# State space rounds of a hybrid decoder step: each tile's sums, scans and rotation in one round, outputs one round behind

## What is computed

```python
u = (h @ w_in).reshape(bsz, t, S5_GROUPS, S5_GROUP)
bu_re = jnp.einsum('btgi,gpi->btgp', u, bb_re)
bu_im = jnp.einsum('btgi,gpi->btgp', u, bb_im)
...
_, _, x_re, x_im = lax.associative_scan(combine, (a_re_t, a_im_t, bu_re, bu_im), axis=1)
y = (jnp.einsum('gip,btgp->btgi', c_re, x_re) - jnp.einsum('gip,btgp->btgi', c_im, x_im)
     + d_skip * u).reshape(bsz, t, S5_WIDTH)
za, zg = jnp.split(jax.nn.gelu(y).astype(h.dtype) @ w_glu, 2, axis=-1)
return za * jax.nn.sigmoid(zg), x_re[:, -1], x_im[:, -1]
```

## Time and profile before

| | |
|---|---|
| three runs | 1793.01, 1790.54, 1792.56 us; median 1792.56 |
| the profiled execution | 1795.36 us, its span 1793.6 us |
| mean granted clock of TensorE | 0.957 of full speed |
| busy share of the span | TensorE 94%, VectorE 78%, ScalarE 67%, POOL 8% |
| the rounds | from 500.07 us (first lags) to 600.92 us (first GLU product) |

### The profile page before, as it was taken

The page is one execution under the profiler, slowest core; times in us unless marked ns, Lnnn a source line. Parts: engine busy times, 40 slices in busy tenths (PEclk is TensorE's granted clock), DMA queues, the critical chain, the costliest instruction groups (busy, mean ns, idle before and its releaser), DMA issues.

```text
span 1793.6 us, 27141 instructions
## 1 busy us (share of the span) xinstructions
PE 1693.6 (94%) x9199; PEld 1423.5 (79%) x9199; DVE 1395.1 (78%) x1587; ACT 1201.2 (67%) x1499; POOL 149.5 (8%) x199
## 2 busy tenths in 40 slices
PE   6989899999787898999999999999999999999994
PEld 3867789988666877888888888888888888888884
DVE  2564454583587546999999999999899999999997
ACT  2633355403474546888888888888887888888885
POOL 1042000000066102500000000000000000000001
PEclk8998899999886898999999999999999999999997
DMA  8662655436361559999999999999999999999995
GB/s 342 274 239 88 227 209 188 159 129 252 128 249 48 199 210 380 422 410 372 381 369 404 365 371 400 371 388 372 368 411 367 361 409 364 399 383 359 396 371 200
DMA packets 72869, 553.22 MB, mean 308 GB/s; under 512 B 8256, under 2 KB 8527, under 8 KB 15328
## 3 DMA queue, kind: packets, MB, share of 16 engines
q1 hardware_dynamic: 69186, 538.54, 77.4%
q0 software_dynamic: 3072, 12.54, 1.9%
q10 hardware_dynamic: 542, 1.20, 0.2%
HBM read 530.74 MB, written 21.53 MB: 308 GB/s over the span
## 4 chain that ended last, share of the span: by engine, by line
PE 89%; DVE 4%; ACT 2%; DMA 2%; POOL 1%; issue 1%; ACTq 0%; DVEq 0%; POOLq 0%; SPq 0%
PE bank L1957 86%; PE bank L2431 2%; DMA arena<-in_state_conv_dram 1%; DMA ring<-in_dense_rows_dram 1%; POOL plain_hi L763 0%; DVE sq L1372 0%; PE bank L2410 0%; DVE rstd L1354 0%; DVE sq L1525 0%; DVE w_lo L469 0%; DMA fT<-y_rows,row_i 0%; ACT w_hi L463 0%; ACT hT L1201 0%; DVE sq L1501 0%; ACT arena L1180 0%
## 5 line engine op out<-in xcount | busy, mean ns | idle before, releaser
L1957 PE MATMUL bank<-w_hi,parts 128*128 128x512 f32 x3024 | 897.2, 391 | 1.5 <-DVE parts L1879 1.5
L516 DVE TENSOR_TENSOR w_lo<-ring,w_hi 128x1024 fp32r<-128x1024 f32 x654 | 785.2, 1223 | 57.0 <-ACT w_hi L511 18.7
L511 ACT ACTIVATE w_hi<-ring 128x1024 fp32r<-128x1024 f32 x654 | 690.6, 1061 | 154.4 <-PE bank L1957 154.3
L1957 PEld LDWEIGHTS bank<-w_hi,parts 128*128 128x128 f32 x3024 | 563.0, 188 | 115.9 <-issue 1.7
L1957 PE MATMUL bank<-w_lo,parts 128*128 128x512 f32 x1512 | 548.2, 390 | 0.0
L1957 PE MATMUL bank<-parts,w_hi 128*128 128x264 f32 x1600 | 312.6, 297 | 23.8 <-DVE parts L1361 23.8
L1957 PEld LDWEIGHTS bank<-w_lo,parts 128*128 128x128 f32 x1512 | 283.8, 188 | 60.0
L1957 PEld LDWEIGHTS bank<-parts,w_hi 128*128 128x128 f32 x1600 | 261.5, 199 | 34.8 <-issue 22.6
L1957 PE MATMUL bank<-parts,w_lo 128*128 128x264 f32 x800 | 234.2, 293 | 0.0
L469 DVE TENSOR_TENSOR w_lo<-ring,w_hi 128x2048 fp32r<-128x2048 f32 x50 | 114.6, 2296 | 147.0 <-ACT w_hi L463 146.9
L1957 PEld LDWEIGHTS bank<-parts,w_lo 128*128 128x128 f32 x800 | 158.1, 198 | 0.0
(11 more groups left out here) (415 smaller groups left out, 1247.7 us busy)
## 6 DMA issues: line engine op xcount, KB each, us to landing
ring<-in_expert_rows_dram SPq DMA_DIRECT2D x330, 1024.0 KB, 7.3
ring<-in_dense_rows_dram SPq DMA_DIRECT2D x48, 2048.0 KB, 8.1
hT<-in_expert_rows_dram SPq DMA_DIRECT2D x55, 1024.0 KB, 7.3
ring<-in_dense_rows_dram SPq DMA_DIRECT2D x8, 1408.0 KB, 6.0
x_rows<-arena SPq DMA_DIRECT2D x1, 7168.0 KB, 27.7
y_rows<-arena SPq DMA_DIRECT2D x10, 512.0 KB, 9.3
arena<-x_rows SPq DMA_DIRECT2D x9, 512.0 KB, 10.0
ring<-in_dense_rows_dram SPq DMA_DIRECT2D x2, 1024.0 KB, 4.8
```

Source lines behind the costliest of these rows:

```text
L511: act.activation(hi_slots[u % AHEAD], raw_unit(u), ACT.Copy).then_inc(hi_ready, 1)
L516: dve.tensor_tensor(lo_slots[u % AHEAD], raw_unit(u), hi_slots[u % AHEAD].bitcast(F32), ALU.subtract).then_inc(lo_ready, 1)
L1957: return pe.matmul(out, lhsT, rhs, start=start, stop=stop, skip_group_check=True)
```

## The change

Each tile is now turned back, has its lags masked, is scanned and rotated in the same round, and its outputs follow one round behind the sums: VectorE and POOL have eight rounds, TensorE and ScalarE nine. On TensorE `outputs(k - 1)` stand between the turns and the lag products of tile k + 1. On VectorE `lags(k)` stand between `turn_back(k)` and `scans(k)`. On POOL `pad_c` is one tile ahead, and `rotate_re(k)` closes round k. On ScalarE `copy_lags(k + 1)` goes from the place behind `b_mats(k + 1)` to the place behind `gelu(k - 1)`, ahead of the copy of an ada block. Ada block 20 goes to round 7, and of the copies back to the order of time those of tiles 4 to 6 go ahead of the last gelu on ScalarE, and are a set of their own on VectorE.

```diff
--- before.py
+++ after.py
@@ -777,17 +777,17 @@
                 step(pool.tensor_tensor(wk[:, 1, :, :], turn_sin[:, k, :, :], wk[:, 2, :, :], ALU.mult))
                 pool.tensor_tensor(x, x, wk[:, 1, :, :], ALU.subtract).then_inc(xre_ready, 1)
 
-            for k in range(KT + 1):
-                if k < KT:
-                    wk = work[k % 2]
-                    pool.tensor_tensor(decay[k % 2], bview(cols[:, 3, 4 * k:4 * k + 4], [P, 4, CHUNKS], 2),
-                                       bview(not_first, [P, 4, CHUNKS], 1), ALU.mult)
-                    pool.wait_ge(w_used, k + 1)
-                    pool.tensor_tensor(wk[:, 0, :, :], wk[:, 0, :, :], wk[:, 1, :, :], ALU.add)
-                    pool.tensor_tensor(wk[:, 2, :, :], wk[:, 2, :, :], wk[:, 3, :, :], ALU.subtract).then_inc(w_ready, 1)
-                    pad_c(k)
-                if k:
-                    rotate_re(k - 1)
+            pad_c(0)
+            for k in range(KT):
+                wk = work[k % 2]
+                pool.tensor_tensor(decay[k % 2], bview(cols[:, 3, 4 * k:4 * k + 4], [P, 4, CHUNKS], 2),
+                                   bview(not_first, [P, 4, CHUNKS], 1), ALU.mult)
+                pool.wait_ge(w_used, k + 1)
+                pool.tensor_tensor(wk[:, 0, :, :], wk[:, 0, :, :], wk[:, 1, :, :], ALU.add)
+                pool.tensor_tensor(wk[:, 2, :, :], wk[:, 2, :, :], wk[:, 3, :, :], ALU.subtract).then_inc(w_ready, 1)
+                if k + 1 < KT:
+                    pad_c(k + 1)
+                rotate_re(k)
 
             pool.wait_ge(s5_out, 2)
             for i, (a, b) in enumerate(((s5_re_prompt, s5_re_sample), (s5_im_prompt, s5_im_sample))):
@@ -1168,10 +1168,9 @@
             copy_lags(0)
             act.wait_ge(acc_full, TILES["in1"] + KT)
             pad_b(1)
-            for k in range(KT + 2):
+            for k in range(KT + 1):
                 if k + 1 < KT:
                     b_mats(k + 1)
-                    copy_lags(k + 1)
                 if k + 2 < KT:
                     pad_b(k + 2)
                 if k in (1, 2):
@@ -1186,19 +1185,26 @@
                 if k < KT:
                     sample_states(k)
                     k_mats(k)
+                if k:
+                    last_states(k - 1)
+                if k == KT:
+                    act.wait_ge(y_used, KT - 1)
+                    for r in range(2):
+                        for s_ in range(4):
+                            act.activation(*from_chunks(slice(4, 7), r, s_), ACT.Copy)
+                if k:
+                    gelu(k - 1)
+                if k + 1 < KT:
+                    copy_lags(k + 1)
                 if k < 4:
                     ada(16 + k)
-                if 1 <= k <= KT:
-                    last_states(k - 1)
-                if k >= 2:
-                    gelu(k - 2)
-                if k == KT:
+                if k == KT - 1:
                     ada(20)
                     split_dense_hi(act, 42)
             act.wait_ge(y_used, KT)
             for r in range(2):
                 for s_ in range(4):
-                    act.activation(*from_chunks(slice(4, 8), r, s_), ACT.Copy)
+                    act.activation(*from_chunks(slice(7, 8), r, s_), ACT.Copy)
             act.activation(hT[0:QUAD, :, TP:T], y_one[0:QUAD, :, 0, :], ACT.Copy)
             act.activation(hT[QUAD:2 * QUAD, :, TP:T], y_one[0:QUAD, :, 1, :], ACT.Copy).then_inc(y_moved, 1)
             ada(21)
@@ -1759,15 +1765,11 @@
                 step(dve.tensor_tensor(wk[:, 3, :, :], turn_cos[:, k, :, :], wk[:, 2, :, :], ALU.mult))
                 dve.tensor_tensor(x, x, wk[:, 3, :, :], ALU.add).then_inc(xim_ready, 1)
 
-            lags(0)
-            for k in range(KT + 1):
-                if k < KT:
-                    turn_back(k)
-                if k:
-                    scans(k - 1)
-                    rotate_im(k - 1)
-                if k + 1 < KT:
-                    lags(k + 1)
+            for k in range(KT):
+                turn_back(k)
+                lags(k)
+                scans(k)
+                rotate_im(k)
                 if 1 <= k <= 2:
                     dve.wait_ge(acc_free, TILES["in1"] + KT)
                     rows_placed = place_rows(slice(4, 8), k - 1)
@@ -1775,16 +1777,17 @@
                         rows_placed.then_inc(u_second, 1)
                 if 1 <= k <= 4:
                     mod_rows(15 + k)
-                if k >= KT - 1:
+                if k >= KT - 2:
                     dve.wait_ge(y_used, 4)
-                    for r in (2 * k - 14, 2 * k - 13):
+                    for r in (2 * k - 12, 2 * k - 11):
                         for s_ in range(4):
                             dve.tensor_copy(*from_chunks(slice(0, 4), r, s_))
             split_dense_lo(dve, 42)
-            dve.wait_ge(y_used, KT)
-            for r in range(2, 4):
-                for s_ in range(4):
-                    dve.tensor_copy(*from_chunks(slice(4, 8), r, s_))
+            for seen, ks in ((KT - 1, slice(4, 7)), (KT, slice(7, 8))):
+                dve.wait_ge(y_used, seen)
+                for r in range(2, 4):
+                    for s_ in range(4):
+                        dve.tensor_copy(*from_chunks(ks, r, s_))
             for r in range(2, 4):
                 ins = dve.tensor_copy(hT[QUAD * r:QUAD * r + QUAD, :, TP:T], y_one[0:QUAD, :, r, :])
             ins.then_inc(y_moved, 1)
@@ -2310,20 +2313,20 @@
             lag_products(0)
             chunk_sums(0)
             turn_lags(0)
-            for k in range(KT + 2):
+            for k in range(KT + 1):
                 if k + 1 < KT:
                     turns_of_b(k + 1)
+                if k:
+                    outputs(k - 1)
+                if k + 1 < KT:
                     lag_products(k + 1)
-                if k >= 2:
-                    outputs(k - 2)
-                if k + 1 < KT:
                     chunk_sums(k + 1)
                     turn_lags(k + 1)
                 if 1 <= k <= 4:
                     ada_rows(15 + k)
                 if k < 4:
                     ada(16 + k)
-                if k == KT:
+                if k == KT - 1:
                     ada(20)
             ada_rows(20)
             ada(21)
```

## The result

The changed kernel takes 1799.51 us (median of 7 runs, 1797.39 to 1802.25) against 1792.56 for the kernel before in the same comparison: 1.0035 of it, 95% interval [1.0022, 1.0047]: slower, by little but clear of the noise. On another chip it took 1800.32, 1.0045 [1.0029, 1.0060]. The profiled run after took 1799.51 (span 1797.8), 4.2 us more than the profiled run before (1795.36), which lay 2.8 above its own median. Of 69 runs of the kernel before on the three chips of the experiments, 37 have a mean granted clock of 0.960 to 0.965 and take 1788.37 to 1793.79 us, and 32, like its profiled run (0.957), have 0.956 to 0.959 and take 1792.71 to 1796.96; all 13 runs of the changed kernel lie at 0.957 to 0.960.

A forecast was written before the change was run, and what follows sets the result against it. No engine bounds the state space rounds throughout (ScalarE, VectorE and TensorE by turns), then TensorE's products do. Rounds 0 to 4 +8.6, tile 5 to first glu product -9.4, first glu tile -0.8: -1.6 us, 1791.0; range 1784.5 to 1798.0.

The forecast's parts named there:

- start: Round 0: VectorE turns back tile 0 at 500.0, lags(0) end at 503.8, the turns of B of tile 2 at 511.0.
- rounds 1 to 4: ScalarE's round and TensorE's block come one after the other; rounds 0 to 4 together cost +8.6 us.
- its signs: VectorE idle before the added rows in rounds 1 to 4, some 4 us in two; tile 5 turned back at 558 to 561.
- rival A: Rounds 0 to 4: TensorE keeps its clock through the pauses, 1785.2 us; chance 0.13.
- rival B: TensorE's clock stays at half from round 4 to the end, slowing rounds 5 and 6, 1798.0 us; chance 0.17.
- Rounds 5 to 7: VectorE's work decides: 8.6 and 12.2 us for tiles 5 and 6, 7.8 for tile 7 until both rotations are done.
- Rival D: Lags beside the additions slow both, tiles 5 to 7 take 1.5 us more each, 1795.5 us; chance 0.08.
- The tail: Last rotation to first glu product: 12.1 us, set by TensorE with the last outputs at half clock.
- First glu tile: Ada block 21 ends ahead of it, so the clock may be up: between 0 and -2.4 us, -0.8 taken.
- Rival C: The rounds keep their length and one is saved whole, 1782.5 us; chance 0.07.

The follow-up runs named there:

- x3_lags0_first: Changed kernel with the lags of tile 0 ahead of the rounds on VectorE, as before the change: 1794.06 us, 1.0002 of the kernel before.
- x4_warm: Changed kernel with TensorE doing the coming ada block's products twice more before the turned lags in rounds 1 and 2: 1790.81 us, 0.9982.
- x5_tail_alone: Kernel before with only the change's tail, ada block 20 ahead of the last outputs and copies in two sets: 1787.20 us, 0.9970.

## Why the prediction was wrong

It said 1791.0; the range ended at 1798.0. The profiled runs differ by +4.2 where it had -1.6, an error of 5.8; 4.1 of it lie in the start and 1.3 in rounds 1 to 4. The other 2.8 to the median came from carrying the offset of the profiled run before over to the result; the one after lay on its median. The offset is that of a run of the kernel before with a low mean clock, and no run of the changed kernel has the higher one; why, no trace shows. Of its signs, VectorE's waits came, but longer (9.65 and 5.55 for some 4), and tile 5 was turned back at 564.34, or 564.9 with 0.5 for the earlier start of after, outside its 553 to 564.

*Start: the step that failed.* It put turns(2), the turns of B of tile 2, at 511.0, at most 512.2 (its terms add up to 511.95). With the 0.5 us added, they ended at 515.1 (513.10 and 1.45): 4.1 over, more than both bounds allowed. Two terms of the sum were too small. lags(0) were taken at the row of a later round, 2.20 with 1.78 for L1744, and took 3.6, with four GpSimd instructions beside them where the later rounds have two: 1.4 us. And TensorE's block behind them, from the lag products to the turns of B, was taken at 7.2, from rows at nearly full speed, and took 9.87, at a clock of 0.50 from 504 to 512: 2.7 us. The prediction allowed here for a half clock in the ada block (1.85 to 3.52) and in part in the chunk sums, and not in the other products. What lowers the clock here stays open: it falls after a pause of 4.29 us, but x3_lags0_first has it at half without that pause, and there the block takes 10.17, a pause of 1.13 included. So the 3.4 us of the stage that this edit gives back are the late start of the block, and the clock's part is not among them.

*Rounds 1 to 4: right.* The chain is as drawn. From R1 to R2 (R1 to R4 are the ends of the ada rows) it is 15.33 us (15.35 forecast), from R3 to R4 9.6 (9.6). Two small misses: R1 0.4 late against the turns of B, and R2 to R3 12.2 for 11.3, since the turns of B took 1.97 at half clock where 1.09 was taken for it. That the clock falls after the pauses of rounds 1 and 2 was right (rival A falls), and that it comes back by round 4 as well: 1.00 from 548 to 564 (rival B falls for the change itself; x4_warm shows a price of 2.9 for one such round, for B's 3.1). The Trainium skill's rule for B (TensorE: Matmul & The Clock Gate, Part 1), that activity releases the throttle, fits the returns at 516 and 592 but not 576 to 592, where TensorE was busy 15.44 of 16.00 us at 0.50.

*Rounds 5 to 7: right.* 8.41, 12.21 and 7.56 from tile to tile and to the scans' end (8.6, 12.2, 7.8). Rival D falls there: L1744 takes 1.58 or 1.59 in each. It was true in round 0 alone, where it wasn't looked for.

*The tail: right in size, by another road.* 11.98 us from the last rotation (592.52) to the glu product, for 12.1. But behind the ada block of 588.27 the clock was at 0.98, so the last outputs took 2.9 and not 5.38, and the bound became VectorE's copies, split and sixteen narrow copies (592.01 to 602.97), the other bound of the tail, put at 10 to 14 and taken to lie nearer to 10.

*First glu tile:* -0.8 taken, -0.3 got (8.12 for 8.45): 0.50 from 604 to 608, with ada block 21 ending 6 us ahead of it where the forecast had its copy 1.5 ahead. x5_tail_alone, where it is 1.7, gets 2.6.

Rival C (a round saved whole) falls with the 14.0 us. That is where the gain of the change went: one round is saved, and the first five are 14.0 us longer together, in the main because the lags are copied behind everything else of ScalarE's round. Copying them early, or taking the ada work out from behind them, gives 12 us and more back, each together with the clock that goes with it.

## What to carry to other kernels

When a step is moved to the end of one engine's round, list what stands behind its consumer on the other in-order queue; putting that work ahead of the late one (a move of two calls in TensorE's program) turned +0.4% into -0.4% to -0.6%. Price the first round of a loop by itself, with what every engine does beside it then: it may have neighbours that the steady rounds have not. And where a change moves TensorE's pauses, price what follows from rows at either clock, in each place: here it fell behind pauses of 4.29, 5.34 and 3.78 us, it held behind one of 2.67 (ada ahead), and with lags(0) first it fell behind 0.37 and 1.13. A profiled run shows one course of the clock; the mean clock of the other runs tells whether it is the common one.

## What was not expected of the hardware

- Four VectorE instructions of 32 x 32 took 0.76 us with GpSimd idle, 1.59 beside two of its additions and 3.24 beside four instructions of it.
- TensorE, busy all the time, stayed at 1.2 GHz for 12 us and more (528 to 540 with the lags early, 12.00 of 12.00 busy), and in the profiled run of an edit that filled the pauses of rounds 1 and 2 it did not fall there, at 524 and 540, but at 556. Of three edits that each shorten the stage alone, by 3.4 to 12.8 us, no joining of two or three was faster than the best one; the clock's course is another in each.
- One kernel's runs on one chip spread by 10 us (1779.62 to 1789.97, ada ahead with lags(0) first), another's by 2 to 3 (ada ahead alone).
